# Layer 1's chunked scan: where the row-constant half of the decay differences is added

## What is computed

```python
def _ssd_scan(xs, dt, a, bm, cm):
    ...
    cs = jnp.cumsum(da, axis=2)
    causal = jnp.tril(jnp.ones((CHUNK, CHUNK), dtype=bool))[:, :, None, None]
    seg = cs[:, :, :, None] - cs[:, :, None, :]
    decay = jnp.exp(jnp.where(causal, seg, -jnp.inf))
    cb = jnp.einsum("bclgn,bcsgn->bclsg", cm, bm)
    y_diag = jnp.einsum("bclsgj,bcsgjp->bclgjp", cb[..., None] * decay, xdt)
    ...
```

## Time and profile before

| what | value |
|---|---|
| median of 3 runs | 1835.37 us (1834.72 to 1836.89) |
| span of the profiled execution | 1835.0 us |
| TensorE busy | 1613.4 us, 88% |
| VectorE busy | 375.5 us, 20% |
| ScalarE busy | 227.1 us, 12% |
| mean granted TensorE clock | 0.948 of full |
| scan of layer 1, first to last step on TensorE | 628.2 to 734.8 us |
| weights moved | 485.78 MB, mean 265 GB/s |

### The profile page before, as it was taken

One profiled execution on the slowest core, in us unless ns is written; L12 is line 12 of the kernel. 1 busy time (PEld: TensorE's weight loads), 2 busy tenths in 40 slices (PEclk: granted clock), 3 DMA queues, 4 the chain that ended last, 5 costly groups with the idle time before them and its releaser, 6 DMA issues.

```text
span 1835.0 us, 25208 instructions
## 1 busy us (share of the span) xinstructions
PE 1613.4 (88%) x10905; PEld 912.3 (50%) x10906; DVE 375.5 (20%) x794; ACT 227.1 (12%) x423; POOL 102.1 (6%) x133
## 2 busy tenths in 40 slices
PE   7877999999999999988789997889869868887886
PEld 5543566667588766463333342345635632323323
DVE  1579120000245434131010010010010010100102
ACT  2410120000221233220000000000000000000001
POOL 5046000000000011000000000000000000000000
PEclk8988999999999999988989998999979989999989
DMA  9444387654463304335998785999949949999995
GB/s 333 165 140 173 138 327 288 225 179 150 147 220 138 138 1 141 135 138 199 397 389 333 302 299 219 398 388 396 393 165 395 389 166 390 395 392 398 388 397 227
DMA packets 216446, 485.78 MB, mean 265 GB/s; under 512 B 12928, under 2 KB 15872, under 8 KB 216320
## 3 DMA queue, kind: packets, MB, share of 16 engines
q1 hardware_dynamic: 206480, 481.51, 70.7%
q10 hardware_dynamic: 9840, 2.33, 0.6%
HBM read 482.78 MB, written 1.05 MB: 264 GB/s over the span
## 4 chain that ended last, share of the span: by engine, by line
PE 68%; DMA 10%; DVE 6%; issue 6%; SPq 6%; ACTq 1%; ACT 1%; POOL 0%; DVEq 0%; POOLq 0%
PE bank L1607 21%; PE bank L1167 19%; PE bank L1638 9%; SPq L422 6%; DMA ring<-in_moe_w_down 5%; DMA ring<-in_moe_w_gate 5%; PE bank L1351 4%; PE bank L1542 3%; PE bank L1461 3%; PE bank L1664 2%; ACTq L521 1%; PE bank L1192 1%; DVE arena L907 1%; DVE arena L915 1%; PE bank L1500 1%
## 5 line engine op out<-in xcount | busy, mean ns | idle before, releaser
L1607 PE MATMUL bank<-ring,arena 128*32 128x256 f32 (+3 forms) x4864 | 519.5, 436 | 114.3 <-issue 65.3
L1607 PEld LDWEIGHTS bank<-ring,arena 128*32 128x32 f32 (+1 forms) x4864 | 231.0, 123 | 395.6 <-issue 294.5
L1167 PE MATMUL bank<-arena,ring 128*128 128x256 f32 x1280 | 287.1, 384 | 1.3 <-ACT arena L632 1.0
L1167 PEld LDWEIGHTS bank<-arena,ring 128*128 128x128 f32 x1280 | 243.9, 193 | 39.2 <-issue 4.5
L1638 PE MATMUL bank<-ring,arena 128*32 128x256 f32 (+1 forms) x2128 | 249.0, 458 | 16.3 <-DMA ring<-in_moe_w_down 14.0
L1126 DVE TENSOR_TENSOR arena<-arena,bank 128x512 f32<-128x512 f32 (+2 forms) x44 | 24.4, 576 | 755.5 <-PE bank L1607 755.5
L1638 PEld LDWEIGHTS bank<-ring,arena 128*32 128x32 f32 (+1 forms) x2128 | 100.5, 120 | 153.7 <-issue 113.4
L741 ACT ACTIVATE arena<-bank 128x512 f32<-128x512 f32 (+2 forms) x44 | 21.1, 508 | 557.3 <-PE bank L1619 557.2
L1351 PE MATMUL bank<-ring,arena 128*128 128x512 f32 x176 | 77.0, 595 | 0.3 <-PE bank L1167 0.3
L1192 PE MATMUL bank<-ring,cT 128*32 128x512 f32 x384 | 54.9, 697 | 10.1 <-ACT cT L574 9.5
L1461 PE MATMUL bank<-ring,arena 128*128 128x512 f32 x128 | 57.7, 593 | 0.3 <-PE bank L1167 0.3
(11 more groups left out here) (263 smaller groups left out, 1161.1 us busy)
## 6 DMA issues: line engine op xcount, KB each, us to landing
ring<-in_moe_w_gate SPq DMA_DIRECT2D x56, 2048.0 KB, 19.5
ring<-in_moe_w_up SPq DMA_DIRECT2D x56, 2048.0 KB, 19.4
ring<-in_moe_w_down SPq DMA_DIRECT2D x56, 2048.0 KB, 19.0
ring<-in_ada_w SPq DMA_DIRECT2D x24, 2048.0 KB, 9.8
ring<-in_m_w_in SPq DMA_DIRECT2D x12, 2048.0 KB, 8.9
ring<-in_ffn_w_gate SPq DMA_DIRECT2D x5, 2048.0 KB, 17.4
ring<-in_ffn_w_up SPq DMA_DIRECT2D x5, 2048.0 KB, 12.0
ring<-in_ffn_w_down SPq DMA_DIRECT2D x5, 2048.0 KB, 8.3
```

The source lines that it names most:

```text
L1167: ins = mm(out_, l, r, start=i == 0, stop=i == len(pairs) - 1, **kw)
L1607: ins = mm(ps[base + b // per][m * h:m * h + m, w * (b % per):w * (b % per) + w], hcur3[:, kc, m * b:m * b + m], sl[at // HALF][:, kc, at ...
```

## The change

Of cs[l] - cs[s], the first term varies along a row of the bank and the second is the same along the whole row (a constant of the partition and the head). Before, a matmul with `ntri` wrote the second. Now VectorE writes the negated cumulative sums once, out of bank 6, into a free row of `hd` (`NCS`), and adds the constant inside the clamp: the single instruction `min(dec, 0)` over 512 columns becomes four over 128 columns, one for each head, each `min(dec + ncs, 0)` with the constant as a scalar operand read from memory. The `ntri` tile and its two GpSimd instructions go. TensorE has a new wait, `ncs_ready`, ahead of `z_part(0)`, since that overwrites bank 6.

```diff
         ident = sb("ident", [P, P])
         tri = sb("tri", [P, P])
-        ntri = sb("ntri", [P, P])
         after = sb("after", [P, P])
...
+        NCS = TMP0
...
-                    (ntri[:, :], -1.0, ALU.is_ge, [[1, P]], -1), (after[:, :], 1.0, ALU.is_gt, [[-1, P]], 1),
+                    (after[:, :], 1.0, ALU.is_gt, [[-1, P]], 1),
...
             dve.wait_ge(s["cs_exp"], 1)
+            c.then(ts(hd[:, NCS], bank(6, 8, NB, HEADS)[:, 2], -1.0, None, ALU.mult), "ncs_ready")
             for n in range(NB * NG):
...
-                c.inc(ts(dmin[:, n % 2], ps[n % 2][:, :], 0.0, None, ALU.min), "dec_min")
+                blk, grp = n // NG, n % NG
+                for j in range(4):
+                    at = 4 * grp + j
+                    ins = ts(dmin[:, n % 2, P * j:P * j + P], ps[n % 2][:, P * j:P * j + P],
+                             hd[:, NCS, blk, at:at + 1], 0.0, ALU.add, ALU.min)
+                c.inc(ins, "dec_min")
...
-                    pe.wait_ge(s["consts"], 12)
+                    pe.wait_ge(s["consts"], 10)
...
             pe.wait_ge(s["cs_exp"], 1)
+            pe.wait_ge(s["ncs_ready"], 1)
             z_part(0)
             pe.wait_ge(s["conv_done"], 32)
...
-                mm(dec, ntri[:, :], da.unsqueeze(2).broadcast_to([P, 4, P]), start=True, stop=False, skip_group_check=True)
                 for j in range(4):
-                    ins = mm(dec[:, j], da[:, j:j + 1].broadcast_to([P, P]), tri[:, :], start=False, stop=j == 3,
-                             skip_group_check=True)
+                    ins = mm(dec[:, j], da[:, j:j + 1].broadcast_to([P, P]), tri[:, :], start=True, stop=True)
```

More of the change, by code:

```diff
@@ L266, in hybrid_trunk @@
             sq_done rg_ready root_in root_done xroot_done out_mm x_ready dve_step             f_mm f_silu f_act
-            dt_mm dt_pre dt_exp dt_ln a_exp da_ready cs_mm cs_exp
+            dt_mm dt_pre dt_exp dt_ln a_exp da_ready cs_mm cs_exp ncs_ready
             xbc_mm conv_done silu_done xs_turned xs_ready b_turned1 btok_ready z_mm z_silu
```

## The result

| what | before | after |
|---|---|---|
| median of the runs made together | 1836.13 us (1834.72 to 1837.54, 4 runs) | 1858.87 us (1857.67 to 1861.28, 4 runs) |
| span of the profiled execution | 1835.0 us | 1858.3 us |
| TensorE busy | 1613.4 us | 1606.5 us |
| first matmul of the first expert | 838.00 | 828.70 |
| from there to the end | 997.0 us | 1029.6 us |

The ratio is 1.0114, with a 95% interval of 1.009 to 1.0138: the change makes the kernel 1.1% slower. TensorE has less work than before, 6.9 us less, and arrives at the experts 9.3 us earlier; the stage behind it then takes 32.6 us more, though nothing in it was edited. 32.6 - 9.3 = 23.3, the difference of the two spans.

The account below looks back on a forecast made before the run. The prediction took TensorE as the bound from step to step in the scan: 13.8 us saved less a 2.2 us wait gives 11.6, so 1835.4 - 11.6 = 1823.8 us, with an 8-in-10 range of 1820.8 to 1829.

Parts of the forecast that it names:

- What goes, 13.8 us: Scan on TensorE: dropping the ntri matmul from 16 steps saves 0.86 us each, 13.8 us, all on the path.
- The bound of 0.11 us a step for weight loads: Scan on TensorE: weight loads might show, 0 to 0.11 us a step; 0 taken; as a rival 1825.6 us, 6%.
- The clamps, +0.68 on VectorE: Scan on VectorE: four clamps take 1.36 us, not 0.68; 1.07 of 1.75 us spare remains, no cost on the path.
- The wait at `z_part(0)`, 2.2 us: Entrance of the scan: TensorE waits for VectorE's negation, starting 2.2 us late (2.0 to 2.3), all on the path.
- The clock behind the gap: Rival, 25%: after TensorE's 2.5 us gap before the scan the clock falls, costing 1.7 us; time 1825.5.
- Two GpSimd instructions fewer ...; 0: Kernel start: two GpSimd instructions fewer, which no one waits for there, change the time by 0.
- A DMA-bound expert stage that starts 11.6 us earlier ends 11.6 us earlier: Expert stage: the 11.6 us gained arrives whole at the end, but for a microsecond or two of clock phase.
- The rival that came true: Rival, 4%: waits before experts' first matmuls lengthen because code lies elsewhere; at 3.5 us each for four, 1837.8 us.

Follow-up runs that it names:

- e4: Kernel after with 16 more warm-up matmuls at TensorE's start and the negation ahead of VectorE's ninth convolution tile; 1824.42 us, ratio 0.992.
- e3: Kernel before with only the clamp cut in four, no scalar term added, the ntri matmul kept; 1837.14 us, ratio 0.9996.
- e1: Kernel after with 16 more warm-up matmuls (64 instructions) at TensorE's start, expert loop at +1 against before; 1831.48 us, ratio 0.996.
- s16: e4 without its padding, plus 16 semaphore increments early on TensorE; expert loop at -47 instructions against before; 1827.34 us, ratio 0.9955.
- s128: e4 without its padding, plus 128 semaphore increments early on TensorE; expert loop at +65 instructions against before; 1870.83 us, ratio 1.0159.
- s0: e4 without its padding; expert loop at -63 instructions against the kernel before; 1854.65 us, ratio 1.0068.
- s32: e4 without its padding, plus 32 semaphore increments early on TensorE; expert loop at -31 instructions against before; 1827.71 us, ratio 0.9921.
- s96: e4 without its padding, plus 96 semaphore increments early on TensorE; expert loop at +33 instructions against before; 1867.89 us, ratio 1.0172.
- s192: e4 without its padding, plus 192 semaphore increments early on TensorE; expert loop at +129 instructions against before; 1862.72 us, ratio 1.0125.

## Why the prediction was wrong, point by point

- **What goes, 13.8 us: right.** 13.76 measured in e4, where nothing else disturbs the scan. The bound of 0.11 us a step for weight loads in the open was rightly left at its lower end.
- **The clamps, +0.68 on VectorE: right in that they cost nothing, too high in size.** 1.12 us in place of 1.36, and the next instruction began 1.03 us behind their start in place of 0.60: 0.43 more, 1.31 to spare and not 1.07. The row of the same shape had two operands from memory; without any it is 0.87 (e3), with one 1.12, with two 1.36.
- **The wait at `z_part(0)`, 2.2 us: right.** 2.52 - 0.30 = 2.22; the negation took 0.21 where 0.2 was taken.
- **The clock behind the gap: the rival held, not the forecast.** 5.37 us in place of 3.67, in the kernel after and in e1 alike: 1.70 us, as that rival priced it. "2.5 lies between, nearer the free one" read the rows by the length of the idle time alone, and they had already shown two outcomes for nearly one length; here the clock fell in both traces that have the gap. So the scan gave 13.8 - 2.2 - 1.7 = 9.9.
- **"Two GpSimd instructions fewer ...; 0": open.** The kernel after gets to layer 1's last convolution products 1.8 us late (612.11, and 610.30 before). It comes from the first 40 us, where TensorE ran at the lower clock for a stretch (granted clock 0.67 from 31 to 37 us, and 1.00 before): 26 of the small matmul records of line 1180 took 4.56 us from 31.79, and 3.07 before. e1, s16 and s128 have the same, e4, s0, s32, s96 and s192 not, all with the same fewer GpSimd instructions, so these don't explain it, and what does is open. 9.9 - 1.8 = 8.1, and 1.2 more is gained between the turn and the first expert: 9.3 in the table.
- **"A DMA-bound expert stage that starts 11.6 us earlier ends 11.6 us earlier": this is the step that failed.** It took the stage as one thing with one bound. The earlier trace rows showed TensorE standing still for 8 to 12 us at an expert's entry, with 3.41 at another, and nothing of DMA behind it. The stage is bound by DMA only while its entries are short; SyncE's queue, which waited 371.0 us for TensorE's gate and up line, waits

```profile
SPq L422 <- PE bank L1612: 467.5, 43, 50.5
```

  in the kernel after (waits of SyncE's queue), 96.5 us longer. The DMA row of the seventh expert's round shows it in tenths of 40 slices, first before (1606 to 1717 us), then after (1624 to 1746 us):

```profile
DMA  9999999999999999999999999999999999999999
```

```profile
DMA  9940069999999999999999999999999999999999
```

  The loads run through without a hole before. After, they go on while TensorE stands still (383 GB/s from 1602 to 1625 us) and dry up behind the stop, from about 1630 to 1642 us. That fits a ring that has filled up in the stop, in which TensorE released no slot.
- **The rival that came true had the right mechanism and the wrong price.** It said that the entries get longer because the code lies elsewhere, and priced it by "the four long ones would have to grow by 11.6 / 4 = 2.9 us each". The long ones did about what they did before (-0.4, +1.6, -1.3 and -0.5 us, in the order of the earlier trace rows); of the four short ones, that of the second expert grew from 3.10 to 4.49 and three from 3.41, 4.98 and 4.63 to 18.82, 10.48 and 18.92, 35.2 us together, with two more stops of 3.56 and 3.38 behind them. A short entry is one whose code is still there, so it is the short ones that have something to lose, and a price of losing it stood in the earlier trace rows too, as the long ones: 12 us and not 3. Even that was low: the long entries at 1112.49, 1359.29 and 1504.01 stood beside DMA engines with little else to do (5 to 89 GB/s), the ones that grew to 18.9 beside a full stream. "Nothing in the rows ties them to an address" had not been looked for in the queue of instruction transfers, whose count by window shows it (2 in the whole round behind the entry of 3.41 us, and none in that entry itself). With that row the chance of 4% could not have stood: nothing said that a shift of 63 in 256 would keep what these entries had, and five of the eight other places tried here lose it, a sixth (-47) in part.

## What to carry to other kernels

Where a kernel has a hardware loop with large branches, look at an engine's idle time put down to issue together with the count of instruction transfers in the same window; if some rounds enter quickly and others slowly, the code's place may decide, as it did here, and any edit ahead of the loop, on that engine, moves it. Judge such an edit only against a version padded back to the old place: here the same arithmetic is 1.1% slower or 0.8% faster than the kernel before, by 64 instructions of padding and one instruction moved. And a wait that is put in front of TensorE costs its length and, as a rival with a good chance, the lower clock behind it.

## What the runs showed of the hardware

- **A stop for instructions is longer beside a full stream of weights.** In the kernel before, the entry of 12.40 us at 1112.49 has five transfers of 16 KB on q8, with the DMAs at 89 GB/s; in the kernel after, the entry of 18.92 us has five too, with the DMAs at 382 GB/s. A short entry of 3.41 us has none. So a transfer adds (12.40 - 3.41) / 5 = 1.8 us in the one and (18.92 - 3.41) / 5 = 3.1 us in the other, estimates by division. That the stream is the reason is argued from these traces, and no run separates it. The stops in the middle of an expert are 0.3 to 3.6 us. In straight code, as in the scan, a fetch isn't seen: 3 transfers on q8 from 628 to 724 us, and no wait for issue.
- **TensorE can keep more than two blocks.** In the kernel before, the 111 us round of an expert has 2 transfers on q8, and none from 1606 to 1695 us. By 1691 us TensorE has run through 332 matmul records of unrolled code there: with their weight loads 664 instructions, and two blocks are 512. The section of the Trainium skill named above gives TensorE's instruction memory as 128 KiB and, further down, says that it is only two blocks; the first is the nearer to this trace. Which blocks stay after a jump, and so why a place of +1 is good and one of +33 bad, is open: no run tells it.
- **VectorE, 128 columns out of a bank:** 281 ns with constants and 341 ns with one scalar from memory, and four in a row 0.87 and 1.12 us; the one of 512 columns 0.68.
